# Two 64-channel score halves on the two row halves of TensorE's array

## The reference, cut to what matters

```
s = einsum('bqhd,bnd->bhqn', q, kc) * scale        # compressed: 32 block keys
p_cmp = masked_softmax(s, cmask)
...                                                # the 16 best blocks of 64 keys are selected
s = einsum('bqhd,bqkd->bhqk', q, kg) * scale       # selected
p_sel = masked_softmax(s, smask[:, None])
...
s = einsum('bqhd,bkd->bhqk', q, kw) * scale        # window of 512 keys
p_win = masked_softmax(s, wmask)
return g[..., 0:1] * o_cmp + g[..., 1:2] * o_sel + g[..., 2:3] * o_win
```

## Time and profile before

| | us |
|---|---|
| median of 3 runs | 3500.89 (3498.96 to 3500.92) |
| profiled execution | 3503.42 |
| its span | 3501.3 |
| TensorE busy, weight loads busy | 3299.0, 1894.1 |
| VectorE, ScalarE, GpSimd busy | 1454.7, 1013.3, 219.8 |
| mean granted clock of TensorE | 0.977 |

### The profile page before, as it was taken

The page is one execution under the profiler, slowest core; times in us unless marked ns, Lnnn a source line. Parts: engine busy times, 40 slices in busy tenths (PEclk is TensorE's granted clock), DMA queues, the critical chain, the costliest instruction groups (busy, mean ns, idle before and its releaser), DMA issues.

```text
span 3501.3 us, 55937 instructions
## 1 busy us (share of the span) xinstructions
PE 3299.0 (94%) x22642; PEld 1894.1 (54%) x22642; DVE 1454.7 (42%) x2792; ACT 1013.3 (29%) x1804; POOL 219.8 (6%) x146
## 2 busy tenths in 40 slices
PE   7999988888899999999999998888888999999998
PEld 4555566666644444444445555666665444444444
DVE  5965643333544311332169556433335533113322
ACT  2123334443533310231112233444443322002211
POOL 0211100000200000000011111000011000000000
PEclk9999999999999999999999998999998999999999
DMA  8423424323221211113153225233313112111322
GB/s 261 119 89 104 130 75 146 122 89 100 76 80 48 66 49 30 48 54 92 50 161 108 86 88 178 81 110 118 127 58 105 43 47 66 48 30 48 78 74 88
DMA packets 376981, 312.52 MB, mean 89 GB/s; under 512 B 122845, under 2 KB 359930, under 8 KB 369658
## 3 DMA queue, kind: packets, MB, share of 16 engines
q1 hardware_dynamic: 369354, 208.60, 21.2%
q0 software_dynamic: 7424, 101.19, 7.7%
HBM read 264.34 MB, written 50.46 MB: 90 GB/s over the span
## 4 chain that ended last, share of the span: by engine, by line
PE 88%; DVE 4%; ACT 3%; issue 2%; DMA 1%; SPq 1%; POOLq 0%; DVEq 0%; ACTq 0%
PE PS L921 44%; PE PS L1038 13%; PE PS L1306 5%; PE PS L1329 5%; PE PS L952 4%; PE PS L1197 3%; PE PS L1013 2%; PE PS L1348 1%; ACT arena L1607 1%; PE PS L1243 1%; PE PS L1204 1%; DVE arena L2200 1%; PE PS L1088 1%; PE PS L999 1%; PE PS L1209 1%
## 5 line engine op out<-in xcount | busy, mean ns | idle before, releaser
L921 PE MATMUL PS<-arena 128*128 128x512 bf16 (+1 forms) x10080 | 1553.9, 318 | 9.9 <-DVE arena L1888 9.9
L921 PEld LDWEIGHTS PS<-arena 128*128 128x128 bf16 x10080 | 754.8, 98 | 808.5 <-issue 16.5
L1038 PE MATMUL PS<-arena 128*128 128x512 f32 (+3 forms) x1152 | 477.6, 570 | 0.0
L1483 ACT ACTIVATE arena<-arena 128x1024 bf16<-128x1024 f32 (+1 forms) x108 | 141.4, 1309 | 1091.6 <-PE PS L921 1080.4
L1038 PEld LDWEIGHTS PS<-arena 128*128 128x128 f32 (+1 forms) x1152 | 208.3, 184 | 236.6 <-issue 203.6
L2514 DVE TENSOR_TENSOR arena<-PS,arena 128x1088 f32<-128x1088 f32 (+1 forms) x48 | 62.0, 1292 | 658.4 <-PE PS L921 634.8
L2205 DVE TENSOR_REDUCE arena<-PS 128x1 f32<-128x1024 f32 (+5 forms) x192 | 138.8, 724 | 379.9 <-PE PS L1309 379.3
L1306 PE MATMUL PS<-arena 128*128 128x512 f32 (+3 forms) x576 | 237.5, 520 | 7.7 <-ACT arena L1616 7.7
L2538 DVE SCALAR_TENSOR_TENSOR arena<-PS,arena 128x1088 f32<-128x1088 f32 x64 | 82.7, 1292 | 354.7 <-PE PS L921 354.2
L1329 PE MATMUL PS<-arena 128*128 128x64 f32 x1632 | 222.3, 284 | 0.0
L1329 PEld LDWEIGHTS PS<-arena 128*128 128x128 f32 x1632 | 210.9, 203 | 5.2 <-DVE arena L2416 1.7
(11 more groups left out here) (352 smaller groups left out, 2864.1 us busy)
## 6 DMA issues: line engine op xcount, KB each, us to landing
arena<-in_w_ff SPq DMA_DIRECT2D x64, 512.0 KB, 4.2
arena<-in_w_ff SPq DMA_DIRECT2D x32, 1024.0 KB, 5.7
arena<-in_cache_nsa_kv SPq DMA_DIRECT2D x256, 64.0 KB
x_s<-arena SPq DMA_DIRECT2D x24, 544.0 KB, 3.5
arena<-x_s SPq DMA_DIRECT2D x2, 4352.0 KB, 13.0
arena<-in_w_in SPq DMA_DIRECT2D x4, 2048.0 KB, 14.7
arena<-in_w_out SPq DMA_DIRECT2D x16, 512.0 KB, 4.2
arena<-in_w_in SPq DMA_DIRECT2D x12, 512.0 KB, 5.8
```

The lines of the kernel that those rows point to most:

```text
L921: last = mm(PS[:, 1536 * k + a:1536 * k + a + wd], ww[:, c, :], xx[:, c, a:a + wd], start=c == 0 and n == 0, stop=c == blocks - 1 and n == 2)
L1038: last = mm(PS[0:r, c * 512:c * 512 + b - a], XNT[:, j, t * P:t * P + r], Wt[:, j, a:b], start=j == 0, stop=j == KD - 1)
L1483: run(WH[k][:, 0:blocks, :], src[k][:, 0:blocks, :], ACT.Copy).then_inc(S["w_hi"], 1)
```

## The change

Scores of the selected and window branches no longer run over 128 rows of which 64 are zero. Queries and keys are now held twice, in partitions 0 to 63 and in 64 to 127. A unit's key blocks are split: the first w = (n + 1) // 2 go to rows 0 to 63 and the first bank of the slot, the rest to rows 64 to 127 and the second bank. Where n is odd and over 1, a matmul of ones with the small tile `FAR` (-1e30 / 64 in each element) fills the missing block of the second bank with -1e30, so that the maximum and the exponential can read both halves as one rectangle. The masks follow, now all after both halves.

To have the channels twice, the transposes of NSA queries and keys become plain float32 matmuls against the identity, one for each half of the output's partitions (`both_halves`). The copies of them now move 128 partitions. The compressed scores use rows 0 to 63 alone. Two of the four memsets go away and a small one for `FAR` comes.

```diff
+        def width_of(u):
+            return (len(keys_of(u)) + 1) // 2
+
+        def scores_of(u):
+            slot = PS[:, (u % 2) * 1024:(u % 2 + 1) * 1024]
+            n, w = len(keys_of(u)), width_of(u)
+            if UNITS[u][1] == "fox" or n == 1 or w == 4:
+                n = n if UNITS[u][1] == "fox" or n == 1 else 8
+                return slot[:, 0:n * P], n
+            return slot.rearrange("p (g n) -> p g n", g=2)[:, :, 0:w * P], 2 * w
...
+                def both_halves(key, src, g):
+                    out = open_group(key)
+                    for j in range(4):
+                        for half in (slice(0, HD), slice(HD, P)):
+                            last = mm(out[half, j * P:(j + 1) * P], src[:, 4 * g + j, :], ident, start=True, stop=True)
+                    last.then_inc(S["pt_T"], 1)
...
-                        transposes(key, KV4[:, :, key[1] // 2 * 2, :], HD, key[1] % 2)
+                        both_halves(key, KV4[:, :, key[1] // 2 * 2, :], key[1] % 2)
...
-                        src, r = ((QN, HD), (QF, AUG), (KF, AUG))[n // 2]
-                        transposes(key, src, r, n % 2)
+                        if n < 2:
+                            both_halves(key, QN, n)
+                        else:
+                            transposes(key, (QF, KF)[n // 2 - 1], AUG, n % 2)
...
-                            last = mm(out[:, i * NPB:(i + 1) * NPB], QNT[key[1] % 2][:, i * P:(i + 1) * P], KVC[:, 512:544],
+                            last = mm(out[:, i * NPB:(i + 1) * NPB], QNT[key[1] % 2][0:HD, i * P:(i + 1) * P], KVC[0:HD, 512:544],
...
-                pe.wait_ge(S["pad_ready"], 4)
+                pe.wait_ge(S["pad_ready"], 3)
+
+                def halves(u, q, kt):
+                    h, kind, i = UNITS[u]
+                    js, w = keys_of(u), width_of(u)
+                    at, rows = [(u % 2) * 1024 + 512 * g for g in range(2)], (slice(0, HD), slice(HD, P))
+                    if 1 < len(js) < 2 * w:
+                        mm(PS[:, at[1] + (w - 1) * P:at[1] + w * P], ones[rows[1]], FAR[rows[1]].to_broadcast([HD, P]), start=True, stop=True)
+                    masks = [(0, wnegb)] * (kind == "win" and i >= 4) + [(len(js) - 1, cnegb)]
+                    for g, part in enumerate((js[:w], js[w:])):
+                        if part:
+                            mm(PS[:, at[g]:at[g] + len(part) * P], q[rows[g], i * P:(i + 1) * P],
+                               kt[rows[g], part[0] * P:(part[-1] + 1) * P], start=True, stop=not any(c // w == g for c, m in masks))
+                    for c, mask in masks:
+                        x = at[c // w] + c % w * P
+                        last = mm(PS[:, x:x + P], identb, mask, start=False, stop=True)
+                    last.then_inc(S["s_mm"], 1)
...
+                    if kind != "fox":
+                        halves(u, q, kt)
+                        return
...
-                    run(PR[u % 2][:, 0:width], PS[:, (u % 2) * 1024:(u % 2) * 1024 + width], ACT.Exp,
+                    y = PR[u % 2][:, 0:n * P]
+                    run(y if len(x.shape) == 2 else y.rearrange("p (g n) -> p g n", g=2), x, ACT.Exp,
...
-                    V.reduce_max(NMX[k][:, v:v + 1], PS[:, (u % 2) * 1024:(u % 2) * 1024 + P * len(keys_of(u))], AX,
-                                 negate=True).then_inc(S["nm_ready"], 1)
+                    x, n = scores_of(u)
+                    V.tensor_reduce(NMX[k][:, v:v + 1], x, AX if len(x.shape) == 2 else mybir.AxisListType.XY, ALU.max,
+                                    negate=True).then_inc(S["nm_ready"], 1)
...
-                for n in range(4):
+                for n in range(2):
                     G.memset(PADDED[HD:P, n * 2 * SEQ:(n + 1) * 2 * SEQ], 0.0).then_inc(S["pad_ready"], 1)
-                pool.wait_ge(S["pad_ready"], 4)
+                pool.wait_ge(S["pad_ready"], 2)
+                G.memset(FAR, NEG / HD).then_inc(S["pad_ready"], 1)
+                pool.wait_ge(S["pad_ready"], 3)
```

More of the change, by code:

```diff
@@ L275, in build_step @@
         KWT = lo.take(SEQ)
+        FAR = lo.take(1)
         VREP = lo.take(P, i=4, n=NPB)
@@ L1301, in scores @@
                         masks = []
-                        if kind == "win" and i >= 4 and a == 0:
-                            masks.append((0, wnegb))
                         if part[-1] == i:
@@ L1590, in group_out @@
                         n = key[1]
-                        run((KST, KWT)[n // 2][0:HD, (n % 2) * 512:(n % 2 + 1) * 512], group_bank(key)[0:HD, :],
-                            ACT.Copy).then_inc(S["pt_evA"], 1)
+                        run((KST, KWT)[n // 2][:, (n % 2) * 512:(n % 2 + 1) * 512], group_bank(key), ACT.Copy).then_inc(S["pt_evA"], 1)
                     elif what == "q":
                         h, n = key[1:]
-                        dst, r = ((QNT, HD), (QFT, AUG), (KFT, AUG))[n // 2]
+                        dst, r = ((QNT, P), (QFT, AUG), (KFT, AUG))[n // 2]
                         if n >= 2:
@@ L1609, in probs @@
                 def probs(u):
-                    width = P * len(keys_of(u))
+                    x, n = scores_of(u)
                     k, v = u // UH_ % 2, u % UH_
@@ L2168, in group_out @@
                         n = key[1]
-                        V.tensor_copy((KST, KWT)[n // 2][0:HD, (n % 2) * 512:(n % 2 + 1) * 512],
-                                      group_bank(key)[0:HD, :]).then_inc(S["pt_evD"], 1)
+                        V.tensor_copy((KST, KWT)[n // 2][:, (n % 2) * 512:(n % 2 + 1) * 512], group_bank(key)).then_inc(S["pt_evD"], 1)
                     elif what == "q":
                         h, n = key[1:]
-                        dst, r = ((QNT, HD), (QFT, AUG), (KFT, AUG))[n // 2]
+                        dst, r = ((QNT, P), (QFT, AUG), (KFT, AUG))[n // 2]
                         if n >= 2:
```

## The result

The median of seven runs of the changed kernel is 3510.68 us (3506.87 to 3516.23), against 3499.58 us for seven runs of the kernel before on the same chip: a ratio of 1.0033, with an interval of 1.0023 to 1.0044. The change is slower by 11.1 us. That lies within the range, but it isn't the "no change" that was named as likeliest: it is rival A's side of it.

The account below looks back on a forecast made before the run. TensorE was taken to bound the kernel. Scores -16.0, transposes +6.8, start +5.4, compressed scores +2.6 and wider readers +2.8 gave +1.6 us, hence 3503 us, no change (3494 to 3508); range 3484 to 3534.

Parts of the forecast that it names:

- rival A: Side costs bite through uncovered transposes (+2.2), wide readers (+5) and lower clock (+7): +14 us more, 3517; chance 0.27.
- Overlap of the halves: Selected and window units: both row halves stream together, saving 47.7 us; an eight-block unit takes about 1.0 us.
- rival B: Passes of the two halves go in program order, the second half starting one pass later: +31 us, 3534; chance 0.05.
- C: Halves that differ in rows alone stream one after the other: +61 us, 3564; chance 0.07.
- Price of the change of form: Tile change into and out of half-row scores, 0.248 us in each of 128 units: +31.7 us (bounds 23 and 40).
- Score terms together: Selected and window scores, streaming saved less tile changes: -16.0 us; with +2.8 for wider maximum and exponential, -13.2.
- Query groups between units: Twelve groups of heads 1 to 3, +0.75 us each, a quarter covered by waits: +6.8 us (bounds +2 and +10).
- Compressed scores: Eight compressed-score groups on half the rows, a tile change in and out, +0.32 us each: +2.6 us.
- Start: Two query and four key groups ahead of each layer's first scores: +2.7 us a layer, +5.4 (bounds +2 and +9).
- Wide readers: Maximum and exponential read one filler block for n = 3, 5 and 7: +2.8 us (bounds 0 and +8).
- Sum without the clock: All terms added, nothing for the clock: +1.6 us, forecast 3503 us, no change; chance 0.43.
- Clock: Attention stretches at 1.2 GHz might grow or shrink: nothing put in the sum, bounds -5 and +15 us.

Follow-up runs that it names:

- e2: Kernel before, with selected and window scores on rows 0 to 63 alone, one matmul after the other, nothing split: 3548.68 us, ratio 1.0134.
- e6: Kernel before, with one tiny bf16 matmul on 64 rows and 8 columns ahead of each selected or window unit: 3542.45 us, ratio 1.0116.
- e1: Kernel before, with NSA queries and keys by matmuls into both halves and compressed scores on 64 rows, other scores untouched: 3520.61 us, ratio 1.0054.
- e10: Kernel before, with matmuls into both halves only in the six groups ahead of each layer's first unit: 3512.97 us, ratio 1.0036.
- e9: Kernel before, with maximum and exponential of units of 3, 5 and 7 blocks reading one block more, no filler: 3502.04 us, ratio 1.0006.
- e4: Changed kernel, with units of one and two key blocks back on the full array: 3498.97 us, ratio 1.0000 to before.
- e8: Changed kernel, with two idle float32 matmuls in each wait ahead of a request's probability transposes: 3500.68 us, ratio 1.0000 to before.
- e11: Changed kernel, small units on the full array, idle matmuls in the requests' waits, ahead of first query groups and of the third unit's scores: 3490.77 us.
- e5: Kernel before, with two idle float32 matmuls in each wait ahead of a request's probability transposes: 3498.13 us, ratio 0.9991.
- e3: Changed kernel, with query groups between units as transposes again and a second copy for the other half: 3510.5 us, ratio 1.0027 to before.

## Why the prediction was right or wrong

- **Overlap of the halves: right.** Pairs 7 ns apart, a five-block unit in 0.85 us and one of eight in 1.06, for the 1.0 that was forecast. Rivals B and C fell. The Trainium skill (TensorE: Matmul & The Clock Gate, Part 3) says that matmuls keep program order in start and end. The starts in the trace agree for matmuls taken whole: the first half's two passes start at 561.194 and 561.408, the second half's at 561.201 and 561.414. What did not hold is the reading of it in rival B, that both passes of one float32 matmul come before the first pass of the next; so it was this reading, and not the rule, that the trace spoke against.
- **Price of the change of form: right.** 0.248 us forecast; a one-block unit is 0.234 longer after, e2 gives 40 us for 160 (0.234 by the timeline), e6 34 us for 128 (0.25, its tiny matmul and its load included).
- **Score terms together: right.** -13.2 with the wide readers forecast, -13.6 measured (after less e1 at equal clock). The scores alone are -18.6 by the timelines for the -16.0 forecast.
- **Query groups between units: over-sized.** The group takes 1.02 us from its first matmul to the next line's, where before had 0.85 for the same distance, wait included. I charged the change out (0.20) as new, but the four transposes before already ran in the form 128*64 and paid it: from their last start to the next line's, where nothing is waited for, it is 0.20 us (0.10 in two cases), and 0.20 after. So a group costs 0.5 to 0.6 more and not 0.75. Of the twelve groups, six stand ahead of no wait and grew by 0.50 to 0.60 us, the other six by 0.14 to 0.27 (from the last matmul ahead of the group to the first behind it): 4.6 us instead of 6.8.
- **Compressed scores: over-sized.** From the first matmul to the second line behind (L1256) 3.25 us, before 3.13 (565.60 to 568.73): +0.12 for 0.32. The eight groups together grew by 0.9 us instead of 2.6.
- **Start: right in the trace** (3.5 and 2.6 us for 2.7 a layer; before has 7.1 and 7.9 us from the first query group to its first scores, after 10.6 and 10.5), with more behind it through the clock in e10.
- **Wide readers: about right,** 3.5 to 5 for 2.8 at equal clock, with no change not excluded (e9).
- **Sum without the clock: right.** +1.6 forecast, +0.7 at equal clock, though the line is no better than 3 to 4 us. The lengths in the timelines (-18.6 + 4.6 + 6.1 + 0.9) give -7.0, and about -3 with the wide readers. Part of the agreement is luck: the scores saved more than forecast, and the side costs on TensorE were smaller in sum (11.6 for 14.8).
- **Clock: the failed step.** The prediction put it as "I take nothing, bounds -5 and +15". It was 0.978 in the mean of before and 0.972 after; at the 1.9 us per 0.001 that before's own executions show, that is 11 us, the whole of the measured difference. So the term that failed is this one: nothing was put in the sum for it, and it measured some 11 us. The sign was argued correctly under rival A ("the stretches of small units carry the pauses and gain nothing"), and e4, e6 and e8 support it: fewer changes of form raise the clock, more lower it with no other edit, and filled waits bring back 10 us. I should have taken the middle of my bounds, not nothing, since the changes of form alone added 256 pauses of 0.09 us to stages where TensorE already fell to 1.2 GHz in places. They are not the only cause: e1 has none of them in its scores and lost 0.003 of clock, and e10, with other groups at the start alone, nearly as much. Of rival A the clock came true, in a larger size (11 for 7), and the uncovered transposes did not.

What is shown: time comes back when waits are filled, with the work of the change untouched and the clock of its stretch back from 0.91 to 0.95 (e8), and it goes when forms change (e6). What is only correlated: the 1.9 us per 0.001, hence the split into terms at equal clock; how the fall of 0.006 divides among the parts of the change is not shown. What is open: why one wait of 1.3 us is followed by the lower clock in one execution and not in another. Before and after have nearly the same waits ahead of 884 us, and only after ran cold behind them. In the timeline of PE, before and then after:
```profile
881.95 0.42 PE L1219 MATMUL PS<-arena 128*32 128x128 f32 x8 [1.28 <-ACT arena L1607]
```
```profile
882.24 0.43 PE L1243 MATMUL PS<-arena 128*32 128x128 f32 x8 [1.38 <-ACT arena L1649]
```

## What to carry to other kernels

Splitting a contraction of 64 over the two row halves pays 0.107 us per 128 columns and pass saved, and costs about 0.25 us for each excursion into the half-row form and back: the unit table shows a gain from four key blocks on, and e4 that units of one and two belong on the full array. In a kernel bound by TensorE, count pauses as well as columns: a change that is neutral in streaming but adds 0.1 us pauses and short units can lose 0.3% through the granted clock. Before judging such a change, look at the mean clock beside the time, fill the engine's known waits with idle matmuls and time again; e11 shows that not every wait pays.

## What was not expected of the hardware

- Work added to the bounding engine made the program faster: 17 us of matmuls, -3.4 us (e5, just clear of noise), and -10 us in after (e8).
- One kernel's executions on one chip range from 3494 to 3528 us with the mean clock from 0.979 to 0.966 (e3). With three such runs a difference of 0.3% can't be judged.
- A change of the clock can fall far from the edit: e10 touches only six of the ten groups at the start of a layer, and in layer two it lost 4 us between 250 and 500 us behind them.
